# Places of their own for the last six value tiles of a decoder layer, with token halves and a last pair of column quarters

## The reference, cut to what matters

```
x = layer_norm(ALPHA * x + mixer(x), ln1_g, ln1_b)
w = gate * gelu(x . u_tab[expert])              # top 16 experts of 8 heads, per token
h = sum over the chosen experts of w * v_tab[expert]
x = layer_norm(ALPHA * x + h, ln2_g, ln2_b)     # mean and variance over the 1024 columns
```

## Time and profile before

| | |
|---|---|
| time, median of 3 runs | 1078.61 us (1077.36 to 1079.89) |
| the profiled execution's own time | 1080.63 us |
| its span, first to last instruction | 1078.8 us |
| granted TensorE clock, mean | 0.996 of full speed |
| PE busy | 1062.0 us, 98% of the span |
| DVE, ACT, POOL busy | 787.6, 609.7, 172.4 us |
| value tiles loaded | 128 x 512 KB |

### The profile page before, as it was taken

The page is one execution under the profiler, slowest core; times in us unless marked ns, Lnnn a source line. Parts: engine busy times, 40 slices in busy tenths (PEclk is TensorE's granted clock), DMA queues, the critical chain, the costliest instruction groups (busy, mean ns, idle before and its releaser), DMA issues.

```text
span 1078.8 us, 17961 instructions
## 1 busy us (share of the span) xinstructions
PE 1062.0 (98%) x5580; PEld 904.1 (84%) x5580; DVE 787.6 (73%) x1511; ACT 609.7 (57%) x1116; POOL 172.4 (16%) x119
## 2 busy tenths in 40 slices
PE   8999999999999999999999999999999999999996
PEld 5888888878888888888888999988888888888885
DVE  4457767577999998999999888875555555555556
ACT  4346646655456656666766666664444555544543
POOL 3040002003000022223323455510000000000001
PEclk9999999999999999999999999999999999999999
DMA  7654444444455554444444444445556655555553
GB/s 244 212 191 167 137 156 149 158 143 156 157 176 193 182 182 165 159 170 158 156 161 147 141 137 150 142 166 192 202 202 207 199 194 194 194 194 192 191 190 109
DMA packets 52857, 186.48 MB, mean 173 GB/s; under 512 B 6336, under 2 KB 6976, under 8 KB 52816
## 3 DMA queue, kind: packets, MB, share of 16 engines
q1 hardware_dynamic: 51152, 181.82, 50.0%
q0 software_dynamic: 944, 3.15, 0.9%
q10 hardware_dynamic: 720, 1.05, 0.3%
HBM read 184.94 MB, written 1.05 MB: 172 GB/s over the span
## 4 chain that ended last, share of the span: by engine, by line
PE 91%; DVE 3%; DMA 2%; issue 1%; POOL 1%; ACT 1%; POOLq 0%; ACTq 0%; SPq 0%; DVEq 0%
PE ps L1490 22%; PE ps L1492 11%; PE ps L1586 10%; PE ps L1587 10%; PE ps L1588 10%; PE ps L1258 6%; PE ps L1260 5%; PE ps L1259 5%; PE ps L1541 5%; PE ps L1319 1%; DVE wlo L791 1%; DMA xraw<-xT 1%; POOL xt L423 0%; PE ps L1506 0%; DMA raw<-w_tiles_v 0%
## 5 line engine op out<-in xcount | busy, mean ns | idle before, releaser
L791 DVE TENSOR_TENSOR wlo<-raw,whi 128x1024 fp32r<-128x1024 f32 x341 | 424.0, 1244 | 240.8 <-ACT whi L485 238.6
L485 ACT ACTIVATE whi<-raw 128x1024 fp32r<-128x1024 f32 x343 | 363.4, 1060 | 283.5 <-DMA raw<-w_tiles_v 166.4
L1490 PE MATMUL ps<-pair,whi 128*128 128x512 f32 x1152 | 412.7, 401 | 0.7 <-DVE wlo L791 0.7
L1492 PE MATMUL ps<-pair,wlo 128*128 128x256 f32 x1152 | 321.4, 279 | 0.0
L1490 PEld LDWEIGHTS ps<-pair,whi 128*128 128x128 f32 x1152 | 216.4, 188 | 48.5 <-DVE wlo L791 1.0
L1492 PEld LDWEIGHTS ps<-pair,wlo 128*128 128x128 f32 x1152 | 217.2, 189 | 0.0
L1586 PE MATMUL ps<-whi,hhi 128*128 128x512 f32 x512 | 199.4, 389 | 1.3 <-DVE wlo L791 1.2
L1588 PE MATMUL ps<-whi,hlo 128*128 128x512 f32 x512 | 199.2, 389 | 0.0
L1587 PE MATMUL ps<-wlo,hhi 128*128 128x512 f32 x512 | 199.2, 389 | 0.0
L462 POOL TENSOR_TENSOR hot_j<-raw_ij,gateT 128x512 f32<-128x512 bf16 x64 | 121.7, 1901 | 332.0 <-DVE raw_ij L1163 332.0
L674 ACT ACTIVATE low<-ps 128x256 f32<-128x256 f32 x144 | 55.1, 383 | 137.3 <-PE ps L1492 135.9
(11 more groups left out here) (212 smaller groups left out, 878.6 us busy)
## 6 DMA issues: line engine op xcount, KB each, us to landing
raw<-w_tiles_u SPq DMA_DIRECT2D x128, 512.0 KB, 3.2
raw<-w_tiles_v SPq DMA_DIRECT2D x128, 512.0 KB, 4.3
raw<-w_tiles_in SPq DMA_DIRECT2D x63, 512.0 KB, 3.2
raw<-w_tiles_q SPq DMA_DIRECT2D x16, 512.0 KB, 3.3
raw<-w_tiles_out SPq DMA_DIRECT2D x8, 512.0 KB, 3.3
xt<-x POOLq DMA_DIRECT2D x1, 1024.0 KB, 8.7
raw<-w_tiles_in SPq DMA_DIRECT2D x2, 256.0 KB, 4.2
xraw<-xT SPq DMA_DIRECT2D x2, 256.0 KB, 8.2
```

Of the source, the lines that this page charges most:

```text
L485: act.activation(whi[:, tile.slot, :], raw[:, tile.slot, :], ACT.Copy)\
L791: dve.tensor_tensor(wlo[:, tile.slot, :], raw[:, tile.slot, :], whi[:, tile.slot, :].bitcast(F32), ALU.subtract)\
L1490: pe.matmul(ps[:, bank, :], whi[:, tile.slot, cols], pair[:, k, :, :].rearrange("p a n -> p (a n)"), start=k == 0, stop=False)
L1492: last = pe.matmul(ps[:, bank, SEQ:2 * SEQ], wlo[:, tile.slot, cols], ahi[:, k, :], start=False, stop=k == KC - 1)
```

## The change

- The last six value tiles (122 to 127) no longer pass through the ring. Each has places of its own (late_raw with late_lo over it, late_hi, late_hhi, late_hlo) in the first 60 rows of H, whose values are used by then.
- SP issues their loads between those of the ring: one behind each eighth ring tile from tile 64 on, so behind tiles 71, 79, 87, 95, 103 and 111. These loads wait for nothing of their own.
- ACT and DVE split them behind ring tiles 111, 113, 115, 117, 119 and 121, two instructions more on each engine for each late tile.
- The ring's 122 tiles are all taken whole (12 matmuls). Then PE takes the six late tiles by token halves: half 0, columns 0 to 511, then 512 to 1023; half 1, columns 0 to 511, then 512 to 767, and at the very end 768 to 1023. The two quarters are matmuls of 256 columns. The last quarter gathers in bank VB[0], which token half 0 has left (PE waits for its variance); what the ring's tiles gave to it stays in VB[3], and DVE adds both.
- DVE takes token half 1 in pieces: column half 0 as one sum with two statistics of 256 columns, then quarter by quarter. Only one addition (256 columns) and one bn_stats (256 columns) stand behind the last matmul ahead of the variance.
- The first LayerNorm does the same work as before. Its statistics buffer has four places instead of two.

```
@@ -85,6 +85,10 @@
 GLA_SQRT, GLA_RMS, Y_FIRST = 58, (59, 60), 61
 GATE_B, GATE_A = (52, 56), 60
 TAIL = 3
+LATE = 6
+LATE_FROM, LATE_EVERY = 64, 8
+RINGED = TILES_V - LATE
+LATE_SPLIT = 111
 Y_TURN, Y_LATE = T_OUT - 1, 1
 BLK = 4
@@ -229,7 +233,7 @@
     ident = place("ident", [P, P])
     keys = place("keys", [P, 2, NK])
     iota = place("iota", [P, P])
-    stats = place("stats", [P, NT, 2, 6])
+    stats = place("stats", [P, NT, 4, 6])
     mv = place("mv", [P, NT, 2])
     rstd = place("rstd", [P, NT])
     shift = place("shift", [P, 1])
@@ -301,6 +305,11 @@
     assert at[0] <= nc.sbuf_usable_end, at[0]
     hhi = place("hhi", [P, NS, SEQ], F32R, alias=hot_at)
     hlo = place("hlo", [P, NS, SEQ], F32R, alias=hot_at + NS * SEQ * 4)
+    late_raw = place("late_raw", [P, LATE, W], alias=work_at)
+    late_lo = place("late_lo", [P, LATE, W], F32R, alias=work_at)
+    late_hi = place("late_hi", [P, LATE, W], F32R, alias=work_at + 4 * LATE * row)
+    late_hhi = place("late_hhi", [P, LATE, SEQ], F32R, alias=work_at + 8 * LATE * row)
+    late_hlo = place("late_hlo", [P, LATE, SEQ], F32R, alias=work_at + 9 * LATE * row)
     g2b = place("g2b", [P, D], alias=act_at)
     b2b = place("b2b", [P, D], alias=act_at + D * 4)
@@ -315,7 +324,7 @@
     PAST_BANK = 4
     OUTB = (6, 7, 0, 1)
...
              "in_ln1 in_ln2 hi_ready lo_ready lo_first_q tiles_used evac_act evac_dve consts "
              "act_split_hi act_split_lo lr_done lr_copied z_done z_read roped mo_tp mo_qk mo_s mo_max "
              "mo_exp mo_pt mo_ptc mo_o mo_out gl_l gl_sum gl_exp gl_tp gl_qk gl_across gl_mm gl_past gl_att "
@@ -327,6 +336,7 @@
     S = {n: nc.alloc_semaphore(n) for n in names}
     raw_full = [S[f"raw_full{n}"] for n in range(NS)]
+    late_full = [S[f"late_full{n}"] for n in range(LATE)]
     in_xT = [S[f"in_xT{n}"] for n in range(X_PARTS)]
     x_parts = [slice(0, 1), slice(1, 2)] + [slice(2 * n, 2 * n + 2) for n in range(1, KC // 2)]
@@ -356,12 +366,23 @@
                          (rope_s[:, :, :], sin), (keys[:, :, :], keysT),
                          (gnorm[:, :], norm_g.to_broadcast([P, GDV]))):
             sp.dma_start(dst, src).then_inc(S["in_small"], 16)
-        for first, n, src, skip in ((0, TILES_IN, w_tiles_in, 1), (T_OUT, TILES_OUT, w_tiles_out, 0),
-                                    (T_Q, TILES_Q, w_tiles_q, 0), (T_U, TILES_U, w_tiles_u, 0),
-                                    (T_V, TILES_V, w_tiles_v, 0)):
-            with sp.Fori(skip, n // NS) as i:
+        def rounds(first, src, begin, end):
+            with sp.Fori(begin // NS, end // NS) as i:
                 for k in range(NS):
                     load(Tile(first + k, i, NS), src[bass.ds(i * NS + k, 1), :, :].rearrange("a p n -> p (a n)"))
+        for first, n, src, skip in ((0, TILES_IN, w_tiles_in, NS), (T_OUT, TILES_OUT, w_tiles_out, 0),
+                                    (T_Q, TILES_Q, w_tiles_q, 0), (T_U, TILES_U, w_tiles_u, 0),
+                                    (T_V, LATE_FROM, w_tiles_v, 0)):
+            rounds(first, src, skip, n)
+        for n in range(LATE):
+            at = LATE_FROM + n * LATE_EVERY
+            rounds(T_V, w_tiles_v, at, at + LATE_EVERY)
+            sp.dma_start(late_raw[:, n, :], w_tiles_v[RINGED + n, :, :]).then_inc(late_full[n], 16)
+        rounds(T_V, w_tiles_v, LATE_FROM + LATE * LATE_EVERY, RINGED // NS * NS)
+        for m in range(RINGED // NS * NS, RINGED):
+            load(Tile(T_V + m), w_tiles_v[m, :, :])
         for half in range(2):
             cols = slice(half * CW, (half + 1) * CW)
             sp.wait_ge(S["out_ready"], half + 1)
@@ -768,10 +789,15 @@
                 act.activation(ps[:, LN2_BANKS[n] + half, :], b[:, half * CW:(half + 1) * CW], ACT.Copy)\
                     .then_inc(S["g2_ready"], 1)
                 value_tiles(LN2_COPIES + 2 * n + half, LN2_COPIES + 2 * n + half + 1)
-        value_tiles(LN2_COPIES + 4, TILES_V // 4 - 1)
-        for m in range(T_END - 4 + AHEAD, T_END):
-            split_h(Tile(m))
-            split_hi(Tile(m))
+        value_tiles(LN2_COPIES + 4, (LATE_SPLIT - AHEAD) // 4)
+        for m in range(LATE_SPLIT, RINGED):
+            split_h(Tile(T_V + m))
+            split_hi(Tile(T_V + m))
+            n, odd = divmod(m - LATE_SPLIT, 2)
+            if not odd:
+                act.activation(late_hhi[:, n, :], H[:, RINGED + n, :], ACT.Copy).then_inc(S["late_hi_ready"], 1)
+                act.wait_ge(late_full[n], 16)
+                act.activation(late_hi[:, n, :], late_raw[:, n, :], ACT.Copy).then_inc(S["late_hi_ready"], 1)
         own.do(act.activation(gate_warm[:, :], ident[:, 0:1], ACT.Sqrt))
         layer_norm(1, 0)
         ln_sqrt(1, 1)
@@ -991,36 +1017,30 @@
             if k == Y_LATE:
                 y_low(2)
                 y_low(3)
-        def norm(n, banks, gain, bank_done, gain_ready, tiles, done):
-            def total(t, half):
-                xs = xt[:, t, half * CW:(half + 1) * CW]
-                own.do(dve.scalar_tensor_tensor(out=xs, in0=xs, scalar=ALPHA, in1=ps[:, banks[2 * t + half], :],
-                                                op0=ALU.mult, op1=ALU.add))
-                own.step(dve.bn_stats(stats[:, t, half, :], xs))
-            def variance(t):
-                own.wait()
-                own.do(dve.bn_aggr(mv[:, t, :], stats[:, t, :, :].rearrange("p a b -> p (a b)")))
-                dve.tensor_scalar(rstd[:, t:t + 1], mv[:, t, 1:2], LN_EPS, None, ALU.add)\
-                    .then_inc(S["ln_var"], 1)
-            dve.wait_ge(S[bank_done], 1)
-            total(0, 0)
-            dve.wait_ge(S["half_done"], n + 1)
-            total(0, 1)
-            variance(0)
+        def total(t, first, width, bank, parts=1):
+            xs = xt[:, t, first:first + width]
+            own.do(dve.scalar_tensor_tensor(out=xs, in0=xs, scalar=ALPHA, in1=bank, op0=ALU.mult, op1=ALU.add))
+            size = width // parts
+            for part in range(first, first + width, size):
+                own.step(dve.bn_stats(stats[:, t, part // size, :], xt[:, t, part:part + size]))
+        def variance(n, t, groups):
+            own.wait()
+            own.do(dve.bn_aggr(mv[:, t, :], stats[:, t, 0:groups, :].rearrange("p a b -> p (a b)")))
+            dve.tensor_scalar(rstd[:, t:t + 1], mv[:, t, 1:2], LN_EPS, None, ALU.add)\
+                .then_inc(S["ln_var"], 1)
+        def scale_first(n):
             dve.wait_ge(S["ln_sqrt"], NT * n + 1)
             own.do(dve.reciprocal(rstd[:, 0:1], rstd[:, 0:1]))
             dve.scalar_tensor_tensor(out=shift[:, :], in0=mv[:, 0, 0:1], scalar=-1.0, in1=rstd[:, 0:1],
                                      op0=ALU.mult, op1=ALU.mult).then_inc(S["ln_shift"], 1)
-            dve.wait_ge(S[bank_done], 2)
-            total(1, 0)
-            dve.wait_ge(S["tiles_used"], tiles)
-            total(1, 1)
-            variance(1)
+        def apply_second(n, gain, gain_ready, done):
             dve.wait_ge(S[gain_ready], 4)
             halves = [slice(half * CW, (half + 1) * CW) for half in range(2)]
             for half, cols in enumerate(halves):
@@ -1045,7 +1065,18 @@
             split_lo(Tile(T_Q + 2))
         dve.wait_ge(S["in_x"], 16)
-        norm(0, OUTB, LN1_BANKS, "x1_bank", "g1_ready", T_Q, "ln_done")
...
         x1_low()
@@ -1236,15 +1267,39 @@
         for k in range(4):
             split_h(Tile(T_V + k + AHEAD))
             split_lo(Tile(T_V + k + AHEAD))
-        with dve.Fori(1, TILES_V // 4 - 1) as i:
+        with dve.Fori(1, (LATE_SPLIT - AHEAD) // 4) as i:
             for k in range(4):
                 tile = Tile(T_V + k, i, 4).plus(AHEAD)
                 split_h(tile)
                 split_lo(tile)
-        for m in range(T_END - 4 + AHEAD, T_END):
-            split_h(Tile(m))
-            split_lo(Tile(m))
-        norm(1, VB, LN2_BANKS, "out_bank", "g2_ready", T_END, "out_ready")
+        for m in range(LATE_SPLIT, RINGED):
+            split_h(Tile(T_V + m))
+            split_lo(Tile(T_V + m))
+            n, odd = divmod(m - LATE_SPLIT, 2)
+            if not odd:
+                dve.wait_ge(S["late_hi_ready"], 2 * n + 1)
+                dve.tensor_tensor(late_hlo[:, n, :], H[:, RINGED + n, :], late_hhi[:, n, :].bitcast(F32),
+                                  ALU.subtract).then_inc(S["late_lo_ready"], 1)
+                dve.wait_ge(S["late_hi_ready"], 2 * n + 2)
+                dve.tensor_tensor(late_lo[:, n, :], late_raw[:, n, :], late_hi[:, n, :].bitcast(F32), ALU.subtract)\
+                    .then_inc(S["late_lo_ready"], 1)
+        for half in range(2):
+            dve.wait_ge(S["value_done"], half + 1)
+            total(0, half * CW, CW, ps[:, VB[half], :])
+        variance(1, 0, 2)
+        scale_first(1)
+        dve.wait_ge(S["value_done"], 3)
+        total(1, 0, CW, ps[:, VB[2], :], 2)
+        dve.wait_ge(S["value_done"], 4)
+        total(1, CW, QW, ps[:, VB[3], 0:QW])
```

(85 more changed lines are left out.)

## The result

The changed kernel takes 1085.34 us (median of 4 runs, 1084.85 to 1086.87), against 1078.68 us of the kernel before. The ratio is 1.0069, with a 95% interval of 1.0057 to 1.0081: 0.7% slower. The prediction was 1075.4 us, with a range of 1074.2 to 1079.0. It had the wrong sign.

What follows compares the result with a forecast made beforehand. PE, busy for 98% of the span, was taken as the bound, with only the tail to win. Removing its 1.74 us stall and shortening DVE's last work gave -3.2 us, so 1078.61 became 1075.4 us, range 1074.2 to 1079.0.

Steps and rivals of the forecast that it cites:

- The matmuls: Tail from tile 122: 54 matmuls at 0.2267 us and 36 at 0.115 make 16.38 us, the last ending at 1068.93.
- The stall of PE: PE's waits for the last tiles at the tail: loading and splitting late tiles early removes 1.74 us.
- The quarters: Last two 256-column pieces of token half 1: 36 matmuls at 0.115 us each, bounds 0.113 and 0.19.
- Rival D: The 256-column matmuls go at the pace of the listed weight loads: 2.7 us more, 1078.1 us; chance 0.07.
- DVE behind the last matmul: Addition and bn_stats of 256 columns ahead of bn_aggr take 0.91 us, before 1.43; bn_aggr starts 2.54 us earlier.
- Token half 0: Its products are complete at 1060.5 us, so its store goes near 1070 and no longer ends last.
- The end: SP's second store issues at 1073.16 and lands at 1075.26; the span ends at 1075.6 against 1078.8, 3.2 us less.
- Loads and splits: Value stage: the six added loads and the ACT and DVE splits hide; uncovered splits cost up to 0.68 us at five places.
- B: A lagging DMA engine costs a little at each late load, up to 3.6 us: 1077.5 us; chance 0.22.
- Rival C: DMA lag does not drain, so late loads stop PE: 9.1 us minus the gain, 1084.5 us; chance 0.12.
- E: Splits of ring tiles 112 to 120 come too late, 0.3 us at five places: 1.5 us, 1076.9; chance 0.07.
- the sum: Whole kernel: -3.2 us, loads and splits hidden; the median of 1078.61 us becomes 1075.4; chance 0.52.

Runs made afterwards that it cites:

- e2: Changed kernel with four small buffers packed into one, so H, hhi and hlo are back at their old addresses; 1076.92 us, ratio 0.9977.
- e8: The same kernel as e2, run again in a later set of runs; 1076.38 us, ratio 0.9977.
- e11: Changed kernel with 192 bytes more ahead of H, so H lies 256 bytes beyond its old address; 1075.99 us, ratio 0.9977.
- e12: Kernel before with every buffer, the ring too, 64 bytes further on; 1078.07 us, ratio 1.0002.
- Experiment 7: e2 with all six late loads issued together behind the load of ring tile 63; 1082.45 us, ratio 1.0040.
- experiment 1: Kernel before with only the larger statistics buffer, half of it unused; 1088.85 us, ratio 1.0089.
- e4: No layer computed: groups of 30 fp32r matmuls, both operands placed at varied bytes from a multiple of 256; 512-column groups at 0.2266 to 0.2331 us a matmul.
- e5: No layer computed: groups of 30 fp32r matmuls, also 512/256-column pairs, only the stationary operand's distance varied; pairs 0.3531 us at distance 0, 0.3469 at 224.

## Why the prediction was wrong

**The step that failed is "The matmuls".** It reads "Before, from tile 122 on, 72 of 512 columns. After, 54 of 512 and 36 of 256: as many columns", and costs these at 0.2267 and 0.115. The 1,464 matmuls of the 122 ring tiles are in no term. They were carried over at the pace of before, because no line of theirs was edited. Their spacing went to 0.2333 us: +9.74 us, which alone turns -2.9 into +6.8. Against the kernel before, the medians differ by 1085.34 - 1078.68 = 6.7. The edit that did it stands in the diff and in the list of changes (stats with four places for two), and the prediction gave it no sentence and no price. Had it been followed through the placement, it would have led to "H, hhi and hlo move by 64 bytes against the ring". No row of before showed a price for that, and a bound from both sides was due.

**The stall of PE (-1.74 us): right for that execution.** PE has no gap up to its last matmul. How much there was to win depends on the landings, see the end below.

**The quarters: near.** 0.120 us each instead of 0.115 (36 x 0.005 = 0.18 us). Rival D is out: they do not go at 0.19.

**DVE behind the last matmul: right.** From the start of the addition to bn_aggr 0.92 us (1077.34 - 1076.42), forecast 0.91. bn_aggr itself took 0.26 instead of 0.21 us, where the forecast had 0.01 more.

**Token half 0: off the path, as forecast.** ACT's stores issue 1.8 us behind the start of PE's last matmul (1077.83 - 1076.03), where the forecast had 1.4 (1070 - 1068.65). The forecast had not seen what holds them: ACT's work on rstd of token half 1 (line 649) stands ahead of them in ACT's program, and ACT had been idle 5.76 us for it. They still issue 2.15 us ahead of SP's and land first.

**The end: -3.2 us forecast, -2.90 in the profiled executions, -1.9 to -2.7 in the timed runs** (e2, e8, e11). The prediction had named the reason for the smaller one. Landings that stay at 4.3 us are in that one trace alone. In e12, a kernel with the same instructions, the load view of line 345, 920 to 1000 us, shows

```profile
DMA to landing us min/median/max: 3.0/3.3/3.5
```

and there PE's stop at the tail is one of 0.6 us. From the start of value tile 122 to the end of the span e12 takes 1076.0 - 1050.42 = 25.58 us, and e11 1073.4 - 1049.87 = 23.53. That is 2.05 us, and the prediction had 2.1 for landings of 3.2 us.

**Loads and splits (B, C, E): hidden, as the sum had it.** In the changed kernel the same view gives, for the ring loads,

```profile
DMA to landing us min/median/max: 3.0/3.3/3.8
```

with late loads landing in 4.2 us, and no wait of PE. Rival C gave 1084.5 us, near the measured 1085.3, but its mechanism did not occur: PE never waited for wlo in the value stage. The number is a coincidence. Experiment 7 shows a stop by queued loads, in a kernel that was made to have it; it happens once and drains. There a load cost 1.27 us, where the prediction had 1.7. The sum was right that the loads hide, but in an easier case than it feared: with landings of 3.3 us a ring tile has some 2.2 us of margin and not 1.09. Whether B, C or E would cost something at landings of 4.3 us stays untested.

**What stays open.** Why the distance of the two addresses modulo 256 bytes sets the spacing, and in this uneven way, is not shown; the runs show only that it does. Nor is it shown why one execution of the kernel before had landings of 4.3 us for 230 us, or why its clock fell at 12.7 us.

## What to carry to other kernels

A buffer that grows moves all that is placed behind it: write down, before and after, the distance between the stationary and the moving operand of every hot matmul, modulo 256 bytes. Then pin it, by placing each group of buffers on a multiple of 256, so that a later edit can't shift it. When a kernel is slower and nothing waits, count instructions in a window in which the engine is always busy and compare the starts of neighbouring matmuls; neither the waits nor the durations show it. And a term "unchanged" in a sum is a claim about addresses too: a placement experiment with no added instruction (experiment 1) is the cheapest way to check it.

## What the runs showed of the hardware

- A 512-column fp32r matmul with its own weight load starts every 0.2267 us (0.2278 in two cases) when stationary and moving operand are a multiple of 256 bytes apart, and every 0.2292 to 0.2340 at the other multiples of 32 (e4, e5). 64 bytes cost this kernel 10 us of 1,079 (e1).
- At 256 columns the order turns: 0.120 us at distances of 0, 128 and 160, and 0.117 to 0.118 at 32, 64, 96, 192 and 224 (e4, e5).
- Six 512 KB loads issued together move at about 415 GB/s, some 1.27 us each (e7). Behind a stop of PE of 4.25 us the granted clock was 0.50 for some 3 us, with matmuls 0.43 us apart, which cost 1.5 us more (e7).
